# A decoder trunk in float32: norm products end by column halves, key operands earlier, key weights held on POOL, gMLP mixing later

## The reference

```python
h = layer_norm(ALPHA * h + mixer(h))                       # layer 0: gMLP, layer 1: RWKV-7
h = layer_norm(ALPHA * h + square(relu(h @ w1)) @ w2)      # w1: 1024 x 4096, w2: 4096 x 1024

# gMLP: z = gelu(h @ w_in); u, v = split(z); v = layer_norm(v)
#       mixed[g] = causal(ws[g]) @ v[:, g] + bs[g]  (8 groups of 128 channels, chunks of 128 tokens)
#       out = (u * mixed) @ w_out
# RWKV-7: xm = x + (shift(x) - x) * mu[m] for six m; r, k, v = three 1024 x 1024 products;
#       decay, a, g through small (LoRA) products; a matrix state per head, token by token;
#       a norm per head, a gate, and a last 1024 x 1024 product
```

## Time and profile before

| | us |
|---|---|
| median of 3 runs (1415.4 to 1419.39) | 1417.61 |
| the profiled execution's own time | 1417.99 |
| its span | 1416.3 |

### The profile page before, as it was taken

One profiled execution on the slowest core, in us unless ns is written; L12 is line 12 of the kernel. 1 busy time (PEld: TensorE's weight loads), 2 busy tenths in 40 slices (PEclk: granted clock), 3 DMA queues, 4 the chain that ended last, 5 costly groups with the idle time before them and its releaser, 6 DMA issues.

```text
span 1416.3 us, 22929 instructions
## 1 busy us (share of the span) xinstructions
PE 1325.3 (94%) x9193; PEld 1083.5 (77%) x9193; DVE 676.1 (48%) x871; ACT 512.4 (36%) x879; POOL 589.5 (42%) x356
## 2 busy tenths in 40 slices
PE   7989999999999979999967999997799999999996
PEld 6878888888888863578756878877679888888885
DVE  3475811112444476344747677782581111244447
ACT  4443233232323222433424566664323232323230
POOL 5344344444444460233714345543434444444440
PEclk9999999999999989999987899998999999999999
DMA  7224243333544322543531012011334333233321
GB/s 268 75 75 134 75 119 103 89 104 88 150 121 116 92 81 81 193 136 122 168 125 32 32 47 70 24 32 46 119 90 120 90 103 92 87 111 96 97 66 60
DMA packets 113278, 139.00 MB, mean 98 GB/s; under 512 B 10370, under 2 KB 86194, under 8 KB 113204
## 3 DMA queue, kind: packets, MB, share of 16 engines
q1 hardware_dynamic: 108596, 121.16, 28.6%
q10 hardware_dynamic: 4608, 16.78, 3.2%
HBM read 123.24 MB, written 14.68 MB: 97 GB/s over the span
## 4 chain that ended last, share of the span: by engine, by line
PE 72%; DVE 17%; ACT 5%; DMA 2%; issue 2%; SPq 1%; POOL 0%; ACTq 0%; DVEq 0%; POOLq 0%
PE bank L1408 34%; PE bank L1460 8%; PE bank L1461 8%; PE bank L1462 8%; DVE a_lo L989 3%; DVE gram L1269 2%; PE bank L1554 2%; DVE x_tok L1017 2%; DVE x_tok L1015 2%; DVE stats L1006 1%; PE bank L1770 1%; PE bank L1654 1%; DVE x_tok L1032 1%; DMA proj<-stage 1%; ACT w_hi L575 1%
## 5 line engine op out<-in xcount | busy, mean ns | idle before, releaser
L403 POOL TENSOR_TENSOR w_lo<-raw,w_hi 128x1024 fp32r<-128x1024 f32 x184 | 455.2, 2480 | 633.7 <-ACT w_hi L575 626.0
L575 ACT ACTIVATE w_hi<-raw 128x1024 fp32r<-128x1024 f32 x184 | 193.5, 1056 | 293.2 <-PE bank L1408 281.3
L1408 PE MATMUL bank<-w_hi,a_hi 128*128 128x512 f32 x896 | 280.1, 394 | 19.7 <-DVE a_lo L989 14.3
L1408 PE MATMUL bank<-w_hi,a_lo 128*128 128x512 f32 x896 | 277.3, 391 | 0.0
L1408 PE MATMUL bank<-w_lo,a_hi 128*128 128x512 f32 x896 | 277.2, 391 | 0.0
L1460 PE MATMUL bank<-xT_hi,w_hi 128*128 128x512 f32 (+1 forms) x640 | 237.0, 370 | 0.0
L1461 PE MATMUL bank<-xT_lo,w_hi 128*128 128x512 f32 (+1 forms) x640 | 236.1, 369 | 0.0
L1462 PE MATMUL bank<-xT_hi,w_lo 128*128 128x512 f32 (+1 forms) x640 | 236.1, 369 | 0.0
L989 DVE TENSOR_TENSOR a_lo<-big,a_hi 128x512 fp32r<-128x512 f32 x64 | 140.7, 2204 | 182.5 <-ACT a_hi L594 179.4
L1408 PEld LDWEIGHTS bank<-w_hi,a_hi 128*128 128x128 f32 x896 | 166.6, 189 | 61.5 <-issue 16.7
L1408 PEld LDWEIGHTS bank<-w_lo,a_hi 128*128 128x128 f32 x896 | 169.0, 189 | 35.6
(11 more groups left out here) (221 smaller groups left out, 1419.0 us busy)
## 6 DMA issues: line engine op xcount, KB each, us to landing
raw<-in_ffn_w SPq DMA_DIRECT2D x128, 512.0 KB, 3.9
raw<-in_rw_w_rkv SPq DMA_DIRECT2D x24, 512.0 KB, 3.6
proj<-stage ACTq DMA_DIRECT2D x24, 512.0 KB, 2.7
raw<-in_gm_w_in SPq DMA_DIRECT2D x16, 512.0 KB, 4.4
early<-proj SPq DMA_DIRECT2D x8, 1024.0 KB, 6.1
raw<-in_gm_w_out SPq DMA_DIRECT2D x8, 512.0 KB, 3.6
raw<-in_rw_w_o SPq DMA_DIRECT2D x8, 512.0 KB, 3.7
late<-proj SPq DMA_DIRECT2D x8, 512.0 KB, 4.1
```

The costliest lines, as they stand in the source:

```text
L403: nc.gpsimd.tensor_tensor(w_lo[:, j, :], raw[:, j, :], w_hi[:, j, :].bitcast(F32), ALU.subtract).then_inc(w_lo_ready, 1)
L575: nc.scalar.activation(w_hi[:, j, :], raw[:, j, :], ACT.Copy).then_inc(w_hi_ready, 1)
L1408: last = nc.tensor.matmul(bank[2 * t + h][:], a[:, j, tok], w[:, j, h * HALF:(h + 1) * HALF], start=start and a is a_hi and w is w_hi, sto ...
```

## The change

The edits, in the order of the program:

1. Mixing: groups 0, 1, 2 follow slab 5 of u, groups 3, 4, 5 follow slab 6, groups 6, 7 follow slab 7; none follows slab 4.
2. The last group of gm_out, down0, rw_out and down1 goes tile by tile and within a tile half by half: four slabs of half 0, then four slabs of half 1. `half_summed` tells DVE of half 0. `slab_used` is counted in half 1 of the last tile. The transposes stand behind slab 1 of half 0.
3. DVE adds half 0, takes its statistics, adds half 1, takes its statistics; each add is now waited for. The last tile's two passes go by halves of 512 columns: both passes of half 0 (`x_half`), both of half 1 (`x_ready`). Transposes of tile 3 and the last output DMA are split in the same way.
4. ACT in `finish_norm` of down0 copies the transposed tile 2 ahead of tile 3's square root.
5. Key: ACT rounds `w_hi` slabs 2 and 3 and `a_hi` slabs 0 and 1 ahead of its wait for the LoRA sums; POOL waits for the last of the LoRA mixes before it makes any `w_lo` of key.

```diff
@@ sync
-            for t in range(TT):
+            for t in range(TT - 1):
                 sp.wait_ge(x_ready, 3 * TT + t + 1)
                 sp.dma_start(out[0, t * P:(t + 1) * P, :], x_tok[:, t, :]).then_inc(stored, 16)
+            for h in range(2):
+                if h == 0:
+                    sp.wait_ge(x_half, len(normed))
+                else:
+                    sp.wait_ge(x_ready, 4 * TT)
+                sp.dma_start(out[0, S - P:S, h * HALF:(h + 1) * HALF], x_tok[:, TT - 1, h * HALF:(h + 1) * HALF]
+                             ).then_inc(stored, 16)
@@ gpsimd
             pool.wait_ge(masks_ready, 1)
+            pool.wait_ge(lora_mixed, 3 * KT)
             low_groups(first_slab["key"] // SLOTS, first_slab["rw_out"] // SLOTS)
@@ scalar, finish_norm
+                    if t == TT - 1 and times is not None and not rounded:
+                        turned(times, 2)
                     std_of(norm, t)
                 if times is not None:
-                    for t in range(2, TT):
+                    for t in range(2 if rounded else TT - 1, TT):
                         turned(times, t, rounded)
@@ scalar, behind finish_norm of down0
+            for j in range(AHEAD, SLOTS):
+                round_weights(0, j, first_slab["key"])
+            for k in range(2):
+                act.wait_ge(x_mixed, k + 1)
+                nc.scalar.activation(a_hi[:, k, :], mix[:, k, :], ACT.Copy).then_inc(a_hi_ready, 1)
             act.wait_ge(lora_summed, 1)
             nc.scalar.activation(low_w[0:LORA, :], bank[4][0:LORA, :], ACT.Tanh).then_inc(low_ready, 1)
@@ scalar, products
                 for t in range(TT):
-                    if (u, t) == (2, 0):
-                        left_operand(0, 0)
                     act.wait_ge(bank_projected, TT * u + t + 1)
...
-                    if k <= KT - SLOTS:
+                    if k <= KT - SLOTS and not (u == 0 and k < SLOTS - AHEAD):
                         ahead(k // SLOTS, k % SLOTS, n0)
-                    if k > 0:
+                    if k > (0 if u else 1):
                         left_operand(u, k)
@@ vector, normalise
+            def normalise(y, var_before, result, between=None, add=None, by_half=False):
                 for h in range(2):
+                    if add is not None:
+                        add(h)
                     last = done.inc(nc.vector.bn_stats(stats[:, h, :], y[:, h * HALF:(h + 1) * HALF]))
...
+                parts = (slice(0, HALF), slice(HALF, D)) if by_half else (slice(0, D),)
+                for n, part in enumerate(parts):
+                    then(nc.vector.scalar_tensor_tensor(y[:, part], y[:, part], mean_var[:, 0:1], gains[:, 0, part],
+                                                        ALU.subtract, ALU.mult))
+                    nc.vector.scalar_tensor_tensor(y[:, part], y[:, part], rstd[:, 0:1], gains[:, 1, part],
+                                                   ALU.mult, ALU.add).then_inc(x_half if n + 1 < len(parts) else result, 1)
@@ vector, residual_norm
+                    def add(h):
+                        if h == 0:
+                            dve.wait_ge(half_summed, normed.index(name) * TT + t + 1)
+                        elif t < TT - 1:
+                            dve.wait_ge(tile_summed, product * (TT - 1) + t + 1)
+                        else:
+                            dve.wait_ge(slab_used, first_slab[name] + COUNT[name])
                         y = x_tok[:, t, h * HALF:(h + 1) * HALF]
+                        then(nc.vector.scalar_tensor_tensor(y, y, ALPHA, bank[2 * t + h][:], ALU.mult, ALU.add))
@@ tensor
+            def half_tile(j, t, h, stop):
+                tok, col = slice(t * P, (t + 1) * P), slice(h * HALF, (h + 1) * HALF)
+                nc.tensor.matmul(bank[2 * t + h][:], a_hi[:, j, tok], w_hi[:, j, col], start=False, stop=False)
+                nc.tensor.matmul(bank[2 * t + h][:], a_hi[:, j, tok], w_lo[:, j, col], start=False, stop=False)
+                return nc.tensor.matmul(bank[2 * t + h][:], a_lo[:, j, tok], w_hi[:, j, col], start=False, stop=stop)
@@ tensor, row_product, last group
                 for t in range(TT):
+                    if name in normed:
+                        for h in range(2):
+                            for j in range(SLOTS):
+                                if t == 0 and h == 0:
+                                    arrived(count // SLOTS - 1, j)
+                                last = half_tile(j, t, h, j == SLOTS - 1)
+                                if t == TT - 1 and h == 1:
+                                    last.then_inc(slab_used, 1)
+                                if turning is not None and t >= 2 and (h, j) == (0, 1):
+                                    turn_x(turning, t - 2)
+                            if h == 0:
+                                last.then_inc(half_summed, 1)
+                        if t < TT - 1:
+                            last.then_inc(tile_summed, 1)
+                        continue
@@ tensor, turn_x
-                if norms is not None:
-                    pe.wait_ge(x_ready, norms * TT + t + 1)
                 for h in range(2):
+                    if norms is not None and (t, h) == (TT - 1, 0):
+                        pe.wait_ge(x_half, norms + 1)
+                    elif norms is not None:
+                        pe.wait_ge(x_ready, norms * TT + t + 1)
@@ tensor, behind slab f of u
-                if f >= KT // 2:
-                    for g in (2 * f - KT, 2 * f - KT + 1):
-                        mix_tokens(g)
+                for g in {5: (0, 1, 2), 6: (3, 4, 5), 7: (6, 7)}.get(f, ()):
+                    mix_tokens(g)
```

More of the change, by code:

```diff
@@ L86, in trunk @@
     row_products = [s[0] for s in stream if s[1] == "rows"]
+    normed = ("gm_out", "down0", "rw_out", "down1")
     SLABS = sum(s[2] for s in stream)
@@ L232, in trunk @@
         a_hi_ready, a_lo_ready = sem("a_hi_ready"), sem("a_lo_ready")
-        tile_summed = sem("tile_summed")
+        tile_summed, half_summed, x_half = sem("tile_summed"), sem("half_summed"), sem("x_half")
         bank_read = sem("bank_read")
@@ L389, in _ @@
                                 load(name, source, i, j)
-            for t in range(TT):
+            for t in range(TT - 1):
                 sp.wait_ge(x_ready, 3 * TT + t + 1)
                 sp.dma_start(out[0, t * P:(t + 1) * P, :], x_tok[:, t, :]).then_inc(stored, 16)
-            sp.wait_ge(stored, 16 * TT)
+            for h in range(2):
[5 more added lines that the diff above has]
+                             ).then_inc(stored, 16)
+            sp.wait_ge(stored, 16 * (TT + 1))
         @block.gpsimd
@@ L1000, in groups @@
                             body(i, j)
-            def normalise(y, var_before, result, between=None):
+            def normalise(y, var_before, result, between=None, add=None, by_half=False):
                 for h in range(2):
+                    if add is not None:
+                        add(h)
                     last = done.inc(nc.vector.bn_stats(stats[:, h, :], y[:, h * HALF:(h + 1) * HALF]))
@@ L1025, in residual_norm @@
                 for t in range(TT):
[L1026 to L1030, removed]
+                    def add(h):
[5 more added lines that the diff above has]
+                            dve.wait_ge(slab_used, first_slab[name] + COUNT[name])
                         y = x_tok[:, t, h * HALF:(h + 1) * HALF]
-                        last = done.inc(nc.vector.scalar_tensor_tensor(y, y, ALPHA, bank[2 * t + h][:],
-                                                                       ALU.mult, ALU.add))
-                    dve.wait_ge(dve_done, last)
+                        then(nc.vector.scalar_tensor_tensor(y, y, ALPHA, bank[2 * t + h][:], ALU.mult, ALU.add))
                     def low_first():
@@ L1039, in residual_norm @@
                     early_low = t == 2 and times is not None and split
-                    normalise(x_tok[:, t, :], (which + 1) * TT + t, x_ready, low_first if early_low else None)
+                    normalise(x_tok[:, t, :], (which + 1) * TT + t, x_ready, low_first if early_low else None,
+                              add, t == TT - 1)
                 if times is not None and split:
@@ L1445, in row_product @@
                             last.then_inc(slab_used, 1)
-                        if turning is not None and t >= 2 and j == 0:
-                            turn_x(turning, t - 2)
                     if t < TT - 1:
```

## The result

The changed kernel takes 1437.32 us (median of 4; the kernel before 1418.25 in the same job): 1.014 times as long, interval 1.0121 to 1.0159. The forecast was 1420.1 with a range of 1409 to 1426. The profiled execution took 1436.57, its span is 1434.8 against 1416.3.

A forecast was written before the change was run, and what follows sets the result against it. The prediction took PE to bound the kernel (72% of the chain), its matmuls unchanged, with only the seams moving; terms of -5.3 + 3.2 + 0.8 + 4.3 - 4.3 + 2.5 + 0.6 + 0.7 gave +2.5, so 1420.1 us, range 1409 to 1426.

The forecast's parts named there:

- Mixing: gMLP mixing: moving it behind slab 5 removes PE's 4.12 us wait and speeds the slow first pair, -5.3 us.
- gm_out: Last group and norm of gm_out: halves make PE wait for operands and delay the count ACT needs, +3.2 us.
- the delay of tanh: LoRA part before key: tanh waits for two mixes stretched by POOL, then the table load, +4.3 us.
- key's start: Start of key: PE's 2.39 us wait at slab 1 and the clock fall behind it go, -4.3 us.
- rw_out: Last group and norm of rw_out: tile 0 ends later and ACT waits longer for the count, +2.5 us.
- New idle times and the clock: +0.7: New 2.3 us waits in gm_out, down0 and down1: half a clock fall, less what rw_out may win, +0.7 us.
- LoRA step: LoRA part before key: early copies make tanh and PE wait for DVE's mixes and the table load, +4.3 us.
- Down0: Norm of down0: halves delay ACT's count, but POOL no longer slows DVE's passes, +0.8 us.
- down1: Norm of down1 and output: second half of tile 0, split passes and halved last DMA, +0.6 us.
- third rival: Clock falls behind each new wait in gm_out, down0 and down1, three falls of 1.7 us: +6.9, 1424.5 us; chance 0.22.
- The first rival: Norms of the products: the count does not hold ACT up, tile 2's square root in time: -8.4, 1409.2 us; chance 0.26.
- The second: LoRA part: POOL does not hold up the mixes, only the table load remains, +1.3 for +4.3: 1417.1 us; chance 0.12.

The follow-up runs named there:

- e8: Kernel before, with six extra ACT tanh ahead of the LoRA tanh, so PE waits idle 4.55 us before the projections: 1437.76 us (1.0132).
- e9: Kernel before, with the same six extra ACT tanh, and 20 extra matmuls keeping PE busy in that wait: 1420.65 us (1.0013).
- e6: Kernel before with only the column halves, last tile normalised by halves and ACT's order in down0: 1432.95 us (1.0108).
- e2: Changed kernel, with ACT making key's first two a_hi behind the four LoRA activations instead of ahead of tanh: 1421.89 us.
- m1: Kernel before with the mixing moved, POOL held until key's second mix, key's slabs 2 and 3 rounded early, a_hi behind LoRA activations, no halves: 1413.9 us (0.9952).
- m3: Kernel before with mixing moved, POOL held to key's second mix, key's slabs rounded early, a_hi behind LoRA activations, last tile normalised by halves: 1411.52 us (0.9954).
- e1: Changed kernel, with POOL held until key's second mix instead of the last LoRA mix: 1434.43 us.
- e4: Kernel before with only POOL's hold and ACT's early rounding of key's operands ahead of tanh: 1429.26 us (1.0068).
- e7: Changed kernel, with ACT's copies of tiles 0 and 1 and tile 2's square root ahead of rounding the next product's slab 0: 1435.22 us.
- m7: Kernel before with mixing moved, POOL held to key's second mix, a_hi behind LoRA activations, column halves, tile 2's square root before slab 0's rounding: 1418.8 us (1.0003).

## Why the prediction was wrong

The mechanisms were right one by one. Mixing, gm_out, the delay of tanh, key's start and rw_out came within 0.7 us of their terms; for rw_out that is luck, as said below. The step that failed is **"New idle times and the clock: +0.7"**. It listed only the 2.3 us waits of the halves and priced every fall at the 1.7 us of the earlier trace rows, taken from dense fp32r products that soon had the clock back. The largest new wait of all, the one my own LoRA step had just produced (PE idle from 558.1 to 563.2), was not in the list. And behind it stand no such products, but 64 float32 matmuls, of which the 32 with 65 rows and the first of the third round ran at half clock: +15.3. Doubling 23.1 us for as long as the clock is down gives the bound that was missing, up to +23. The rows of before held a warning too: the wait of 4.12 us ahead of the mixing had a slow first pair behind it, and the mixing term counts 1.72 us for it, but the clock's term names only 590.24 and 1061.30. e8 and e9 settle the cause: 17 us hang on PE's idleness alone.

Point by point for the rest:
- *Down0, +2.6 for +0.8; down1, +2.5 for +0.6.* The same step again: in both the clock fell behind the 2.25 us wait in tile 0 (down1 in the rows at 1403; down0 in the stretch below, where 0.21 of 8 us is 1.7 us of work). That was my third rival, with 0.22, true in two of its three seams. In gm_out it did not fall, and the seam cost 3.5 for 3.2.

```profile
496.00:504.00 8.00, 6.32 (x21) 5.06 (x22) 3.90 (x5) 0.00 (x0) 6.40 (x26) 0.79 0.23 67
```

- *rw_out, +2.6 for +2.5.* Two things that the term left out nearly cancel: the new low stretch (0.28 of 12 us, 3.4 us of work, part of it hidden by the waits) and the fall at 1062 that is gone (1.7 us).
- *The halves as a whole.* Their price was right in kind, low in size: four seams cost 11.2 in the changed kernel (3.5 + 2.6 + 2.6 + 2.5) for a forecast of 7.1, and 14.2 alone (e6), where POOL works beside down0's norm.
- *The first rival (ACT not held up, 0.26)* was wrong: ACT waited 6.95 in gm_out, down0 and rw_out. *The second (mixes undisturbed)* as well: 4.63.
- *The output by halves* ended the kernel 2.5 us after the last pass, 3.1 before: 0.6 saved, where I took 0.3. By the Trainium skill, DMA: Bandwidth & Descriptors, "Anatomy of one DMA", half of 512 KB saves an estimated 0.6, and the trace agrees, though the section describes transfers issued by GpSimd and these are issued by SP.
- *The table load* took 1.28, with tanh 1.29 behind its start, as in the earlier trace rows. The longer switch of the Trainium skill, ScalarE: Activation LUTs, "What ACT_TABLE_LOAD costs", does not show here.

## What to carry to other kernels

Where a change makes TensorE wait, look at what runs behind the wait, not only at how long it is: here a wait of 5 us ahead of 32 float32 matmuls with 65 rows cost that whole stretch at half clock. A few matmuls with no use in the wait may be the cheapest repair (17 us here for 20 matmuls). List every new wait that your own sum produces, and ask of each whether the clock may fall. And an instruction moved ahead in a queue takes its waits with it: here a copy that waited for VectorE held up the activation that TensorE was waiting for.

## What the runs showed of the hardware

- The length of a short wait does not settle whether the clock falls. Ahead of the projections, behind 0.77 us, it fell in the profiled execution of e2 (2.5 us into the first round) and not in those of the kernel before, e6, m1 or m3; behind 1.79 it did not in the profiled one of e1; behind 4.55 to 5.01 it did in all four profiles (changed kernel, e4, e7, e8). The times of e1 and e2 lie in two groups, those of the changed kernel and of e4 in one (1436.6 to 1439.4, and 1427.4 to 1433.6).
- In all seven traces with a fall in the projections, whenever it began, the clock came back 3.9 to 5.2 us into the third round, the first matmuls of 128 rows. The low stretch was 10 us long in m1 and m3, where it began late, and 27 to 34 in the others, nearly all of it with PE busy without a break. So float32 as such does not keep the clock down. The rows are what sets the rounds apart in these records, but no run changed the rows alone.
- The WKV part, full of small waits, took 282.5 to 297.4 us from the end of value to rw_out's first wait for `a_lo`, with the same instructions (284.3 in the kernel before, 282.5 in the changed one, 297.4 in m7, where the granted clock was 0.77 from 940 to 990 against 0.90 before). The length goes with the time at the lower clock: 65 us of it in the changed kernel, 72 in the kernel before, 102 in m7. Kernels that differ only ahead of it are spread by this, and one profile is not enough to tell 5 us apart.
